# Attention probabilities turned by head pairs on two sets of 64 rows, copied by two engines

## The reference, cut to what matters

```python
def hybrid_mixer(h, w_in, gla_w_gate_up, gla_b_gate, gla_out_norm, attn_out_norm, w_out):
    proj = h @ w_in
    aq, ak, av, gq, gk, gv, gr, g_low = jnp.split(proj, cuts, axis=-1)
    ...
    a_out = dilated_attention(aq, ak, av)      # softmax over keys t, t-d, ..., merged patterns
    a_out = rmsnorm(a_out, attn_out_norm)
    o = gla_chunked(gq, gk, gv, log_alpha)
    g_out = rmsnorm(o, gla_out_norm) * jax.nn.silu(gr)
    return jnp.concatenate([a_out, g_out], axis=-1) @ w_out
```

## Time and profile before

| | us |
|---|---|
| median of 3 runs | 1155.17 |
| lowest and highest run | 1154.89 and 1155.43 |
| profiled execution, its own time | 1155.43 |
| its span, from first to last instruction | 1153.6 |
| TensorE busy in it | 1141.0 (99%) |
| VectorE, ScalarE busy | 784.4 (68%), 601.7 (52%) |

### The profile page before, as it was taken

The page is one execution under the profiler, slowest core; times in us unless marked ns, Lnnn a source line. Parts: engine busy times, 40 slices in busy tenths (PEclk is TensorE's granted clock), DMA queues, the critical chain, the costliest instruction groups (busy, mean ns, idle before and its releaser), DMA issues.

```text
span 1153.6 us, 18795 instructions
## 1 busy us (share of the span) xinstructions
PE 1141.0 (99%) x7018; PEld 933.2 (81%) x7018; DVE 784.4 (68%) x1154; ACT 601.7 (52%) x889; POOL 51.2 (4%) x86
## 2 busy tenths in 40 slices
PE   9999999999999999999999999999999999999998
PEld 7987888888868888888777788888887778888886
DVE  6788666558897865554789777566466977765641
ACT  5455544425964554442566665445347576554530
POOL 0120000000001000000100100000010011000000
PEclk9999999999999999999999999999999999999999
DMA  9656877645724687764576169777548534977650
GB/s 342 227 188 212 272 218 216 211 151 186 248 93 146 210 265 218 215 213 151 169 246 196 35 197 291 220 214 226 165 147 273 166 94 146 284 217 218 215 168 37
DMA packets 189066, 228.03 MB, mean 198 GB/s; under 512 B 16497, under 2 KB 132889, under 8 KB 188992
## 3 DMA queue, kind: packets, MB, share of 16 engines
q1 hardware_dynamic: 183600, 215.10, 59.1%
q10 hardware_dynamic: 5040, 11.64, 3.1%
q0 software_dynamic: 352, 0.30, 0.2%
HBM read 212.29 MB, written 1.06 MB: 185 GB/s over the span
## 4 chain that ended last, share of the span: by engine, by line
PE 47%; DVE 2%; ACT 1%; issue 0%; ACTq 0%; POOL 0%; POOLq 0%; DVEq 0%
PE ps L664 15%; PE ps L666 14%; PE ps L665 14%; DVE w_lo L1696 1%; PE ps L1054 1%; PE ps L1111 1%; ACT w_hi L1290 0%; PE ps L1136 0%; PE ps L858 0%; PE ps L1084 0%; PE ps L1103 0%; PE ps L1100 0%; DVE nbuf L2019 0%; PE ps L1083 0%; PE ps L877 0%
## 5 line engine op out<-in xcount | busy, mean ns | idle before, releaser
L1696 DVE TENSOR_TENSOR w_lo<-raw,w_hi 128x1024 fp32r<-128x1024 f32 x377 | 447.6, 1220 | 118.2 <-ACT w_hi L1290 115.3
L1290 ACT ACTIVATE w_hi<-raw 128x1024 fp32r<-128x1024 f32 x377 | 383.2, 1056 | 153.0 <-DMA raw<-w_down 34.7
L664 PE MATMUL ps<-w_hi,a_hi 128*128 128x512 f32 x991 | 390.2, 394 | 2.3 <-DVE w_lo L1696 1.3
L666 PE MATMUL ps<-w_hi,a_lo 128*128 128x512 f32 x991 | 386.0, 389 | 0.0
L665 PE MATMUL ps<-w_lo,a_hi 128*128 128x512 f32 x991 | 385.7, 389 | 0.0
L664 PEld LDWEIGHTS ps<-w_hi,a_hi 128*128 128x128 f32 x991 | 186.0, 188 | 43.4 <-DVE w_lo L1696 2.2
L666 PEld LDWEIGHTS ps<-w_hi,a_lo 128*128 128x128 f32 x991 | 186.0, 188 | 39.4
L665 PEld LDWEIGHTS ps<-w_lo,a_hi 128*128 128x128 f32 x991 | 186.1, 188 | 37.3
L664 PE MATMUL ps<-w_hi,h_hi 128*128 128x512 f32 x480 | 188.4, 393 | 0.5 <-DVE h_lo L2197 0.4
L665 PE MATMUL ps<-w_lo,h_hi 128*128 128x512 f32 x480 | 186.9, 389 | 0.0
L666 PE MATMUL ps<-w_hi,h_lo 128*128 128x512 f32 x480 | 186.8, 389 | 0.0
(11 more groups left out here) (224 smaller groups left out, 777.4 us busy)
## 6 DMA issues: line engine op xcount, KB each, us to landing
raw<-ffn_w_in SPq DMA_DIRECT2D x176, 256.0 KB, 4.0
raw<-w_in SPq DMA_DIRECT2D x96, 256.0 KB, 3.6
raw<-ffn_w_out SPq DMA_DIRECT2D x88, 256.0 KB, 3.2
raw<-w_gate SPq DMA_DIRECT2D x88, 256.0 KB, 3.4
raw<-w_up SPq DMA_DIRECT2D x88, 256.0 KB, 4.1
raw<-w_down SPq DMA_DIRECT2D x88, 256.0 KB, 3.3
moved<-turned SPq DMA_DIRECT2D x176, 64.0 KB, 2.6
raw<-od_w_in SPq DMA_DIRECT2D x40, 256.0 KB, 3.6
```

The costliest lines, as they stand in the source:

```text
L664: nc.tensor.matmul(ps[:, bank, :], hi, wh, start=first, stop=False)
L666: return nc.tensor.matmul(ps[:, bank, :], lo, wh, start=False, stop=last)
L1290: nc.scalar.activation(w_hi[:, v.slot, :], raw[:, v.slot, :], ACT.Copy).then_inc(w_high, 1)
L1696: V.tensor_tensor(w_lo[:, v.slot, :], raw[:, v.slot, :], w_hi[:, v.slot, :].bitcast(F32), ALU.subtract).then_inc(w_low, 1)
```

## The change

In the two "hyb" layers alone, the turning of the probabilities is regrouped by pairs of heads.

- `pair_turn` replaces two `head_turn`: 12 half transposes, those of rows 0 to 63 of both heads into bank 6 and those of rows 64 to 127 into bank 7. It waits for the exponentials of both heads, and for both copies of the pair before.
- `pair_copy` runs on both engines for every pair: ScalarE copies bank 6 (queries 0 to 63 of each 128), VectorE bank 7 (queries 64 to 127), 384 columns each, into every other group of 64 columns of the destination. Each waits for the whole pair's turn. There are four on each engine and layer, as before.
- A second destination, `probsT2`, lies over `qk_moved`, which is free by then; pairs use `probsT` and `probsT2` in turn.
- `head_values` and `last_values` wait for both engines' copies (`pair_out`).
- TensorE's order changes: `pair_turn` 1 comes between `head_values` 0 and 1, `pair_turn` 2 after `head_values` 2, `pair_turn` 3 between `head_values` 4 and 5. `head_values` 5 is then the last step ahead of `turn_y`.
- ScalarE's and VectorE's orders keep their places: each `turned_weights` becomes the `pair_copy` of its pair.

The diff (blank lines inside the new functions left out; `last_values` changes as `head_values` does):

```diff
-        qk_moved, _ = place("qk_moved", [P, 4, 2, 4, NT, 32], F32)
+        qk_moved, at_moved = place("qk_moved", [P, 4, 2, 4, NT, 32], F32)
+        probsT2, _ = place("probsT2", [P, 2, 3 * P], F32, at_moved)
...
-        p_even, p_odd_a, p_odd_v = stage("p_even", HEADS // 2, attn), stage("p_odd_a", HEADS // 2, [1]), stage("p_odd_v", HEADS // 2, hyb)
+        p_even, p_odd = stage("p_even", HEADS // 2, [1]), stage("p_odd", HEADS // 2, [1])
+        p_upper, p_lower = stage("p_upper", HEADS // 2, hyb), stage("p_lower", HEADS // 2, hyb)
...
+        def pair_out(eng, l, j):
+            eng.wait_ge(p_upper.sem, p_upper.at(l, j))
+            eng.wait_ge(p_lower.sem, p_lower.at(l, j))
+        def pair_turned(r):
+            return tb[:, 2 + r, 0:6 * GROUP].rearrange("p (f j) -> p f j", j=GROUP)
+        def pair_weights(j, r):
+            pT = (probsT, probsT2)[j % 2][:, :, :].rearrange("p h n -> p (h n)")
+            return pT.rearrange("p (f r j) -> p f r j", r=2, j=GROUP)[:, :, r, :]
+        def turned_of(l, h):
+            return probsT[:, h % 2, :] if LAYERS[l] == "odd" else (probsT, probsT2)[h // 2 % 2][:, h % 2, :]
...
+            def pair_turn(l, j):
+                pe.wait_ge(weighed.sem, weighed.at(l, 2 * j + 1))
+                if j:
+                    pair_out(pe, l, j - 1)
+                for h in (2 * j, 2 * j + 1):
+                    for i in range(3):
+                        for r in range(2):
+                            group = slice(GROUP * r, GROUP * (r + 1))
+                            tr = nc.tensor.transpose(pair_turned(r)[:, 3 * (h % 2) + i, :],
+                                                     probs[group, h % N_PROBS, P * i:P * (i + 1)], ident[group, group])
+                tr.then_inc(p_turned.sem, 2)
...
             def head_values(l, h, both=True):
-                pe.wait_ge(p_out(l, h).sem, p_out(l, h).at(l, h // 2))
+                if LAYERS[l] == "odd":
+                    pe.wait_ge(p_out(l, h).sem, p_out(l, h).at(l, h // 2))
+                else:
+                    pair_out(pe, l, h // 2)
                 cols = slice(HD * h, HD * (h + 1))
-                pT = probsT[:, h % 2, :]
+                pT = turned_of(l, h)
...
                 linear_values(l, 1, range(1, GLA_H))
-                head_turn(l, 0)
-                head_turn(l, 1)
+                pair_turn(l, 0)
                 pair_logits(l, 2)
                 head_values(l, 0)
+                pair_turn(l, 1)
                 head_values(l, 1)
-                head_turn(l, 2)
-                head_turn(l, 3)
                 pair_logits(l, 3)
                 head_values(l, 2)
-                head_turn(l, 4)
+                pair_turn(l, 2)
                 head_values(l, 3)
-                head_turn(l, 5)
                 head_values(l, 4)
+                pair_turn(l, 3)
                 head_values(l, 5)
-                head_turn(l, 6)
-                head_turn(l, 7)
                 turn_y(l, g_normed, 0, (0,))
                 last_values(l)
                 turn_y(l, g_normed, 0, (1,))
...
+            def pair_copy(l, j):
+                act.wait_ge(p_turned.sem, p_turned.at(l, 2 * j + 1))
+                if j >= 2:
+                    act.wait_ge(attended.sem, attended.at(l, 2 * j - 3))
+                nc.scalar.activation(pair_weights(j, 0), pair_turned(0), ACT.Copy).then_inc(p_upper.sem, 1)
...
                 weights(l, 2)
-                turned_weights(l, 0)
+                pair_copy(l, 0)
                 weights(l, 3)
                 linear_squares(l, 1)
-                turned_weights(l, 2)
+                pair_copy(l, 1)
                 weights(l, 4)
                 weights(l, 5)
-                turned_weights(l, 4)
+                pair_copy(l, 2)
                 weights(l, 6)
                 weights(l, 7)
-                turned_weights(l, 6)
+                pair_copy(l, 3)
...
                     if j == 1:
-                        turned_weights(l, 1)
+                        pair_copy(l, 0)
                         output_gate(l, 1)
                         continue
                     if j == 2:
                         linear_norm(l, 0)
-                    turned_weights(l, 2 * j - 1)
+                    pair_copy(l, j - 1)
                 linear_norm(l, 1)
-                turned_weights(l, HEADS - 1)
-
-            def turned_weights(l, h):
-                dve.wait_ge(p_turned.sem, p_turned.at(l, h))
-                if h >= 2:
-                    dve.wait_ge(attended.sem, attended.at(l, h - 2))
-                V.tensor_copy(probsT[:, h % 2, :], tb[:, 2 + h % 2, 0:3 * P]).then_inc(p_odd_v.sem, 1)
+                pair_copy(l, HEADS // 2 - 1)
+
+            def pair_copy(l, j):
+                dve.wait_ge(p_turned.sem, p_turned.at(l, 2 * j + 1))
+                if j >= 2:
+                    dve.wait_ge(attended.sem, attended.at(l, 2 * j - 3))
+                V.tensor_copy(pair_weights(j, 1), pair_turned(1)).then_inc(p_lower.sem, 1)
```

More of the change, by code:

```diff
@@ L546, in p_out @@
         def p_out(l, h):
-            return p_even if h % 2 == 0 else p_odd_a if LAYERS[l] == "odd" else p_odd_v
+            return p_even if h % 2 == 0 else p_odd
+        def pair_out(eng, l, j):
[8 more added lines that the diff above has]
+            return probsT[:, h % 2, :] if LAYERS[l] == "odd" else (probsT, probsT2)[h // 2 % 2][:, h % 2, :]
         def right(ap, m):
@@ L1112, in head_turn @@
                 tr.then_inc(p_turned.sem, 1)
+            def pair_turn(l, j):
[9 more added lines that the diff above has]
+                tr.then_inc(p_turned.sem, 2)
             def last_values(l):
                 for h in (HEADS - 2, HEADS - 1):
-                    pe.wait_ge(p_out(l, h).sem, p_out(l, h).at(l, h // 2))
+                    if LAYERS[l] == "odd":
+                        pe.wait_ge(p_out(l, h).sem, p_out(l, h).at(l, h // 2))
+                    else:
+                        pair_out(pe, l, h // 2)
                     cols = slice(HD * h, HD * (h + 1))
-                    mm = in_groups(0, probsT[:, h % 2, 0:P], 0, cols, True, True)
+                    mm = in_groups(0, turned_of(l, h)[:, 0:P], 0, cols, True, True)
                 mm.then_inc(tile_attended.sem, 1)
```

## The result

The changed kernel took 1158.61 us (median of 8 runs, 1157.29 to 1159.02), the kernel before 1155.61 beside it (8 runs, 1154.70 to 1156.69): a ratio of 1.0021, with a 95% interval of 1.0012 to 1.0030. By the ratio that is 2.4 us slower, where 2.36 was forecast. The medians alone lie 3.0 apart, each kernel's runs spreading over some 2 us, and the kernel before is at 1155.61 here where it had 1155.17 when I forecast; from these two the absolute 1157.5 is 1.1 us short, and the measured median lies 0.2 us inside the upper end of the range (1158.8). The interval leaves out 1.0000, so the kernel did become slower, but it reaches to both sides of the 0.2% that the prediction called the least difference that can be told: whether it is slower by that much stays open, as the even split of the main case had it. The profiled execution took 1157.29 us, with a span of 1155.5.

The account below looks back on a forecast made before the run. It took ScalarE and TensorE as side by side at their limit in the two "hyb" stretches; 0.73 (ScalarE's stand) + 0.45 (tail) = 1.18 us a layer, 2.36 in all, gave 1155.17 + 2.36 = 1157.5 us, range 1155.6 to 1158.8.

Parts of the forecast that it names:

- the even split of the main case: Whole kernel: main case 0.74, 1156.9 to 1158.1 us; its 2.36 lies on the 2.31 us line, so slower 0.42, same 0.32.
- ScalarE is the bound of the stretch beside TensorE: Stretch in each "hyb" layer: ScalarE busy 10.30 of 10.30 us from first to last exponential, beside TensorE at its limit.
- The rival of TensorE alone: In the stretch, TensorE alone bounds and ScalarE's waits find room: 1.45 us a layer less, 1152.3 in all; chance 0.09.
- The stand before pair 2's copy: ScalarE after exponential 5 waits through pair 2's whole turn, standing 0.73 us, with exponentials 6 and 7 queued behind.
- The rival that only this stand arrives: Only ScalarE's wait for pair 2 reaches the end, or half of both is hidden: 0.6 a layer, 1156.4; chance 0.08.
- the tail: From exponential 7's read to the transpose of g_o: 0.05 + 0.53 + 0.47 = 1.05 us, before 0.60, so 0.45 more.
- Head 5's values and the last turn: After exponential 7: pair 3's turn takes 0.53 us, then head_values(5) 0.47, both ahead of the transpose of g_o.
- The sum: Per "hyb" layer: 0.73 of ScalarE's stand plus 0.45 behind exponential 7 make 1.18 us, two layers 2.36.
- The terms: Per pair, 12 half transposes take 0.53 us and land after 0.62; copies stay 0.49 and 0.55; TensorE saves 1.27 per layer.
- the rival of disturbed copies: Two engines' copies into one tile disturb each other, or strided writes cost: two layers 1.0 us more, 1158.5; chance 0.05.
- The clock rival: TensorE's clock falls in the stretch as it stands more often: 2 us more a layer, 1161.5; chance 0.04.
- the list of TensorE's stands: TensorE's waits after: some 0.3 before pair 1, 0.3 before pair 2, 0.2 before head 4's values, 1.2 before pair 3, 0.3 at end.

## Why the prediction was right

**ScalarE is the bound of the stretch beside TensorE.** Right. Its window is 10.3 us in each kernel whose order leaves it no stand, with full turns, half turns or a third of the turning left out, and taking 0.97 us of squares out of it moved it to 9.5. The rival of TensorE alone is answered by the same runs, above all by the one with less turning.

**The stand before pair 2's copy**: forecast 0.73 us later, measured 641.80 - 631.21 = 10.59 against 9.83 before, 0.76. Undoing its cause alone returned 0.80. The rival that only this stand arrives falls too: with the tail's order alone undone 0.35 came back.

**Head 5's values and the last turn**: forecast 0.45 for the tail; the transpose of g_o starts 13.87 after the first logits matmul, before 12.66, that is 1.21 in all, of which 0.76 is the stand and 0.45 the tail.

**The sum**: 1.18 a layer forecast, 1.21 and 1.22 measured, 2.43 in all against 2.36. The single terms agree with the traces as the sum does, so the agreement is not luck.

**The terms**: 12 half transposes land after 0.62 to 0.63 us as forecast. Their slot is 0.51 (644.09 to 644.60, forecast 0.53), and only 0.42 where the next matmuls have the same 64-row form (635.99 to 636.41): so about half of the fixed 0.18 that I had found in groups of 8 and 16 goes with the change of form behind them. TensorEngine Tiling (Array Packing), Key Properties, in the Trainium skill, says that a change of tiling mode drains TensorE; the trace agrees, at about 0.1 us. My count of such changes was low, 13 on either side where the timelines have 18 before and 18 after, but they cancel all the same. By the distances of starts the turns cost TensorE 1.35 us less in the first layer (3.31 before, 1.96 after), where I had 1.27; most of the rest is pair 0, whose half transposes took 0.42 and not 0.53. The copies stayed at 0.49 and 0.56 us, also for pair 2, where both start at 641.80, so the layout is free and the rival of disturbed copies had nothing. The clock rival neither: 1.00 in both stretches.

**What was off**: the list of TensorE's stands. I had some 0.3 before pair 2's turn; the profile shows 0.59 before head 2's values (640.53), which need VectorE's copy of pair 1. I had worked out that these values end late and yet left the wait ahead of them out of the list. It cost nothing, as pair 2's turn waited for exponential 5 anyway, though only for 0.17 us more. And the absolute time was off by 1.1 us: 0.44 by the level of the series (1155.61 against 1155.17), the rest because the medians of 8 runs lie 3.0 apart where the stretches have 2.43. No step of the chain accounts for this rest.

## What to carry to other kernels

When an engine's work is made cheaper by grouping, write down each neighbour's queue around the new, later release: the transposes here were a third cheaper, and joining two heads put a full round trip of transposing into the one queue that had no rest. A share of the whole span (TensorE 99%) doesn't say which engine sets a stretch; a window cut from an engine's first to its last instruction of a kind tells more: here it showed ScalarE at 10.30 of 10.30 beside TensorE at 10.12, and the runs told the two apart. Where a grouped step must wait for the last of its inputs, put other work of the waiting engine between (exponential 6 ahead of the copy gave back 0.80 of the 1.21 us), and keep steps that are ready out of the way behind it.

## What the runs showed of the hardware

- A half transpose (64 rows by 128 columns) costs 0.03 us in a row and a full one 0.11 ((0.81 - 0.48) / 3), so two halves cost 0.06 in place of 0.11.
- The same 12 half transposes occupy TensorE for 0.42 us before matmuls on 64 rows and 0.51 before matmuls on 128 rows and 32 columns. A 128x512 output matmul takes 0.32 to 0.34 us next to a transpose on 64 rows and 0.23 otherwise.
- From the end of ScalarE's read of a sum to the first transpose that waits for it 0.05 us pass in the odd layer before, and 0.05 to 0.06 at the turns of pairs 2 and 3 after.
- The kernels reached their first stretch at 631.2 to 633.1 us in their profiles, through instructions that are the same in all of them, while a kernel's two stretches agree to 0.01 us. For a change of 1 us in a kernel of 1155, its own stretch is the better measure than the span.
